# Spatial-gate products over both token chunks, the last expert's last w1 piece in two half loads, its two hidden banks closed one by one, and the final norm's roots behind all sigmoids

## What is computed

```python
# branch A: per head group g (8 of 128 channels) and per chunk of 128 tokens
mixed = jnp.einsum("gts,bnsgc->bntgc", w, v) + b_s.T[:, :, None]
return u * mixed.reshape(bsz, seq, SGU_WIDTH)
...
# 32 experts, top 4 of 32 per token
hid = xb @ w1[e] + b1[e]
glu, lin = jnp.split(hid, 2, axis=-1)
glu = jnp.minimum(glu, SWIGLU_LIMIT)
lin = jnp.clip(lin, -SWIGLU_LIMIT, SWIGLU_LIMIT)
act = glu * jax.nn.sigmoid(SWIGLU_ALPHA * glu) * (lin + 1)
return act @ w2[e] + b2[e]
...
hp = rms_norm(x, ple_norm[i])
x = x + jax.nn.sigmoid(hp @ w_ple_gate[i]) * (p[i] @ w_ple_proj[i])
return rms_norm(x, final_norm)
```

## Time and profile before

| | |
|---|---|
| median of 3 runs | 1232.53 us (1232.52 to 1234.2) |
| the profiled execution's own time | 1233.96 us |
| its span | 1232.2 us |
| TensorE busy | 1201.3 us, 97% of the span |
| VectorE, ScalarE, GpSimd busy | 395.3, 226.7, 45.1 us |
| DMA | 459.51 MB, 90.6% of 16 engines' span |
| chain that ended last | PE 79%, DMA 16%, ACT 2%, DVE 1% |

### The profile page before, as it was taken

The page is one execution under the profiler, slowest core; times in us unless marked ns, Lnnn a source line. Parts: engine busy times, 40 slices in busy tenths (PEclk is TensorE's granted clock), DMA queues, the critical chain, the costliest instruction groups (busy, mean ns, idle before and its releaser), DMA issues.

```text
span 1232.2 us, 15135 instructions
## 1 busy us (share of the span) xinstructions
PE 1201.3 (97%) x6239; PEld 641.4 (52%) x6239; DVE 395.3 (32%) x692; ACT 226.7 (18%) x340; POOL 45.1 (4%) x32
## 2 busy tenths in 40 slices
PE   8999999999999999999999999999999999999987
PEld 7988888875444444444444444444434444444336
DVE  2679954642121111221121111122221111112236
ACT  4766654350000000000000000000000000000018
POOL 6600000010000000000000000000000000000000
PEclk9999999998999999999999999999999999999999
DMA  8655488778999999999999999999999999999990
GB/s 269 203 171 206 137 286 327 275 303 338 425 428 427 430 427 429 429 427 429 429 427 429 429 427 430 428 427 430 428 427 430 426 427 429 427 428 427 428 385 35
DMA packets 62088, 459.51 MB, mean 373 GB/s; under 512 B 7353, under 2 KB 16961, under 8 KB 37218
## 3 DMA queue, kind: packets, MB, share of 16 engines
q1 hardware_dynamic: 62050, 458.95, 90.6%
HBM read 457.87 MB, written 1.06 MB: 372 GB/s over the span
## 4 chain that ended last, share of the span: by engine, by line
PE 79%; DMA 16%; ACT 2%; DVE 1%; issue 1%; SPq 0%; ACTq 0%; DVEq 0%
PE bank L986 28%; PE bank L1035 15%; DMA wring<-in_w_dram 12%; PE bank L948 8%; PE bank L700 5%; PE bank L702 5%; PE bank L701 5%; PE bank L957 4%; DMA vz<-in_w_dram 3%; PE bank L994 1%; DMA blk<-in_w_in_dram 1%; PE bank L756 1%; PE bank L759 1%; PE bank L1016 1%; PE bank L763 1%; PE bank L687 1%
## 5 line engine op out<-in xcount | busy, mean ns | idle before, releaser
L986 PE MATMUL bank<-wring,hT 128*64 128x512 f32 x1376 | 308.2, 597 | 7.0 <-DMA wring<-in_w_dram 6.0
L986 PEld LDWEIGHTS bank<-wring,hT 128*64 128x64 f32 x1376 | 96.3, 137 | 198.6 <-issue 181.6
L1836 DVE TENSOR_SCALAR xbcT<-bank 128x512 f32<-128x512 f32 x32 | 22.1, 692 | 420.5 <-PE bank L994 420.5
L1035 PE MATMUL bank<-wring,xbcT 128*64 128x512 f32 x688 | 154.4, 595 | 1.6 <-DVE hT L1800 1.0
L948 PEld LDWEIGHTS bank<-xbcT,ga 128*128 128x128 f32 x1024 | 122.5, 196 | 3.9 <-DVE xbcT L1795 1.2
L948 PE MATMUL bank<-xbcT,ga 128*128 128x64 f32 x1024 | 121.2, 278 | 0.7 <-DVE xbcT L1795 0.7
L1355 ACT ACTIVATE xbcT<-xbcT 128x512 f32<-128x512 f32 x32 | 20.2, 631 | 504.6 <-DVE xbcT L1836 504.6
L1035 PEld LDWEIGHTS bank<-wring,xbcT 128*64 128x64 f32 x688 | 47.6, 137 | 102.9 <-issue 100.1
L1851 DVE COPY xbcT<-bank 128x256 f32<-128x256 f32 x32 | 13.6, 424 | 272.8 <-PE bank L964 272.8
L1490 DVE TENSOR_TENSOR blk_lo<-blk,blk_hi 128x2048 fp32r<-128x2048 f32 x32 | 73.0, 2288 | 38.7 <-ACT blk_hi L1170 38.6
L1360 ACT ACTIVATE xbcT<-bank 128x512 f32<-128x512 f32 x32 | 19.1, 597 | 346.7 <-PE bank L1035 346.7
(11 more groups left out here) (283 smaller groups left out, 1096.0 us busy)
## 6 DMA issues: line engine op xcount, KB each, us to landing
wring<-in_w_dram SPq DMA_DIRECT2D x129, 2048.0 KB, 33.0
blk<-in_w_dram SPq DMA_DIRECT2D x42, 2048.0 KB, 32.2
vz<-in_w_dram SPq DMA_DIRECT2D x21, 2048.0 KB, 32.9
blk<-in_w_in_dram SPq DMA_DIRECT2D x28, 1024.0 KB, 5.2
blk<-in_w_branch_a_dram SPq DMA_DIRECT2D x4, 1024.0 KB, 5.5
blk<-in_w_branch_b_dram SPq DMA_DIRECT2D x4, 1024.0 KB, 6.6
blk<-in_w_out_dram SPq DMA_DIRECT2D x4, 1024.0 KB, 5.1
x<-in_x_dram SPq DMA_DIRECT2D x4, 512.0 KB, 5.1
```

The costliest lines, as they stand in the source:

```text
L986: last = mm(bank[dh * SLOTS:(dh + 1) * SLOTS, :], xgT[:, k, :], at(c)[:, kk * 2 * F + off + dh * W:kk * 2 * F + off + (dh + 1) * W], start ...
L1035: last = mm(YB[dh * SLOTS:(dh + 1) * SLOTS, :], actT[:, kk * P + c * SLOTS:kk * P + (c + 1) * SLOTS], at(W1C + c)[:, kk * D + dh * W:kk * ...
L1836: ts(g_sb, GLU[:, :], LIMIT, None, ALU.min).then_inc(g_done, 1)
```

## The change

1. **Mixing.** The units become `("mix", q)` for q of 0 to 3. Each holds two head groups over both token chunks: two products with 256 columns instead of four with 128, and VectorE takes each group in one instruction over both chunks.
2. **Last piece of w1.** Piece 3 of the last expert comes in two loads of 1 MB, one per contraction slice, each with a semaphore of its own (`last_half`). TensorE starts on the first slice when the first half is there.
3. **Banks closed one by one.** In every expert, GLU's bias product follows its last contraction slice at once, ahead of LIN's last products, and signals for itself; LIN's follows at the end. VectorE waits for each bank separately.
4. **Tail.** ScalarE does all five sigmoids before the one switch to the square root table; `root(0, 1)` moves behind the last sigmoid. The first 512 columns of both token tiles are now premultiplied on VectorE and scaled on ScalarE, `finish` does columns 512 to 1023 of each tile, and the output goes out in four stores of 256 KB.
5. Semaphores are merged to make room (`eps_set` and `dsel_set` into `small_set`, `pool_step` into `consts`), with the same meaning.

```diff
-    u += [("mix", c, h) for c, h in two]
+    u += [("mix", q) for q in range(SGU_HEADS // 2)]
...
                 sp.wait_ge(chunk_used, g - NSLOT + 1)
-                load_chunk(g)
+                if g == NCH * E - 3:
+
+                    r = (W1C - 1) * RW1 * P
+                    src = w1[0, E - 1, r:r + RW1 * P, :].rearrange("(p k) n -> p k n", k=RW1)
+                    for k in range(RW1):
+                        load(slots[g % NSLOT][:, k * 2 * F:(k + 1) * 2 * F], src[:, k, :], last_half[k])
+                else:
+                    load_chunk(g)
...
             for t in range(TT):
-                sp.wait_ge(out_ready, t + 1)
-                if t:
-                    sp.wait_ge(half_ready, 1)
-                sp.dma_start(out[0, t * P:(t + 1) * P, :], xn[:, t, :]).then_inc(stored, 16)
-            sp.wait_ge(stored, 16 * TT)
+                for part, ready in ((slice(W, D), out_ready), (slice(0, W), half_ready)):
+                    sp.wait_ge(ready, t + 1)
+                    sp.dma_start(out[0, t * P:(t + 1) * P, part], xn[:, t, part]).then_inc(stored, 16)
+            sp.wait_ge(stored, 16 * 2 * TT)
...
+            for q in range(SGU_HEADS // 2):
+                name = ("mix", q)
+                wait_empty(pe, name)
+                for i in range(2):
+                    g = 2 * q + i
+                    last = mm(bank_of(name)[:, i * TOKENS:(i + 1) * TOKENS], sgu_wT[:, g, :], v[:, :, g * P:(g + 1) * P],
+                              start=True, stop=True)
+                last.then_inc(full(name), 1)
...
                 for c in range(W1C):
-                    arrived(c)
+                    if not (last_one and c == W1C - 1):
+                        arrived(c)
                     for kk in range(RW1):
+                        if last_one and c == W1C - 1:
+                            pe.wait_ge(last_half[kk], 16)
+                        hidden(c, kk, GLU, 0)
+                        if c == W1C - 1 and kk == RW1 - 1:
+                            pe.wait_ge(aux_done, j + 1)
+                            if first:
+                                pe.wait_ge(b1_low, 2)
+                            bias(0, GLU).then_inc(hid_filled, 1)
+                        last = hidden(c, kk, LIN, F)
                     last.then_inc(chunk_used, 1)
-                pe.wait_ge(aux_done, j + 1)
-                if first:
-                    pe.wait_ge(b1_low, 2)
-                for g, bank in enumerate((GLU, LIN)):
-                    last = mm(bank[:, :], esel[:, :], b1_pair[:, g * W:(g + 1) * W], start=False, stop=True,
-                              skip_group_check=True)
+                last = bias(1, LIN)
                 last.then_inc(hid_filled, 1)
...
             sigmoid(0, W, W, 3, banks[2])
+            square(0, W, W, 1, 3)
+            sigmoid(1, W, W // 2, 4, banks[3])
+            square(1, W, W // 2, 1, 4)
+            sigmoid(1, W + W // 2, W // 2, 5, banks[4])
             fn(table_out[:, 6:7], ones[:, 0:1], ACT.Sqrt)
-            square(0, W, W, 1, 3)
             root(0, 1)
-            fn(table_out[:, 7:8], ones[:, 0:1], ACT.Sigmoid)
-            sigmoid(1, W, W // 2, 4, banks[3])
-            sigmoid(1, W + W // 2, W // 2, 5, banks[4])
-            fn(table_out[:, 0:1], ones[:, 0:1], ACT.Sqrt)
-            square(1, W, W // 2, 1, 4)
             square(1, W + W // 2, W // 2, 2, 5)
             root(1, 2)
...
-            act.wait_ge(x3_rstd, TT)
-            act.wait_ge(spread_done, 1)
-            fn(xn[:, 1, 0:W], sg[:, 1, 0:W], ACT.Copy, scale=rstd3[:, 1:2]).then_inc(half_ready, 1)
+            for t in range(TT):
+                act.wait_ge(x3_rstd, t + 1)
+                act.wait_ge(spread_done, t + 1)
+                fn(xn[:, t, 0:W], sg[:, t, 0:W], ACT.Copy, scale=rstd3[:, t:t + 1]).then_inc(half_ready, 1)
...
-                dve.wait_ge(hid_filled, j + 1)
+                dve.wait_ge(hid_filled, 2 * j + 1)
                 ts(g_sb, GLU[:, :], LIMIT, None, ALU.min).then_inc(g_done, 1)
+                dve.wait_ge(hid_filled, 2 * j + 2)
                 ts(lin_sb, LIN[:, :], LIMIT, -LIMIT, ALU.min, ALU.max).then_inc(loop_step, 1)
...
             dve.wait_ge(x3_done, 2)
-            tt(sg[:, 1, 0:W], x[:, 1, 0:W], fnorm[:, 0:W], ALU.mult).then_inc(spread_done, 1)
+            for t in range(TT):
+                tt(sg[:, t, 0:W], x[:, t, 0:W], fnorm[:, 0:W], ALU.mult).then_inc(spread_done, 1)
             dve.wait_ge(x3_sq, 2)
             ts(part3[:, 0:1], ssq3[:, 0, 0:1], 1.0 / D, RMS_EPS, ALU.mult, ALU.add).then_inc(x3_part, 1)
             embedded(0, W, W, 3)
-            dve.wait_ge(x3_root, 1)
-            nc.vector.reciprocal(rstd3[:, 0:1], rstd3[:, 0:1]).then_inc(x3_rstd, 1)
-            dve.wait_ge(x3_rstd, 1)
-            dve.wait_ge(x3_done, 3)
-            finish(0, slice(0, D))
             embedded(1, W, W // 2, 4)
-            embedded(1, W + W // 2, W // 2, 5)
             dve.wait_ge(x3_sq, 4)
             link(tt(part3[:, 1:2], ssq3[:, 1, 0:1], ssq3[:, 1, 1:2], ALU.add))
             ts(part3[:, 1:2], part3[:, 1:2], 1.0 / D, RMS_EPS, ALU.mult, ALU.add).then_inc(x3_part, 1)
+            embedded(1, W + W // 2, W // 2, 5)
```

More of the change, by code:

```diff
@@ L332, in build @@
         ssq_done = sem("ssq_done")
-        eps_set = sem("eps_set")
+        small_set = sem("small_set")
         root_done = sem("root_done")
@@ L382, in build @@
         loaded = [sem(f"loaded{i}") for i in range(NSLOT)]
+        last_half = [sem(f"last_half{k}") for k in range(RW1)]
         chunk_used = sem("chunk_used")
@@ L730, in natural @@
                                 between()
[L732 removed]
+            pe.wait_ge(consts, 2)
             pe.wait_ge(mix_loaded, 16)
@@ L979, in expert, with hidden, bias @@
                 pe.wait_ge(xg_done, j + 1)
+                def hidden(c, kk, bank, off):
+                    k = RW1 * c + kk
+                    for dh in range(2):
+                        last = mm(bank[dh * SLOTS:(dh + 1) * SLOTS, :], xgT[:, k, :],
+                                  at(c)[:, kk * 2 * F + off + dh * W:kk * 2 * F + off + (dh + 1) * W],
+                                  start=(k == 0), stop=False, skip_group_check=True)
+                    return last
+                def bias(g, bank):
+                    return mm(bank[:, :], esel[:, :], b1_pair[:, g * W:(g + 1) * W], start=False, stop=True,
+                              skip_group_check=True)
                 for c in range(W1C):
-                    arrived(c)
+                    if not (last_one and c == W1C - 1):
+                        arrived(c)
                     for kk in range(RW1):
[L983 to L988, removed]
-                    last.then_inc(chunk_used, 1)
-                pe.wait_ge(aux_done, j + 1)
-                if first:
-                    pe.wait_ge(b1_low, 2)
-                for g, bank in enumerate((GLU, LIN)):
-                    last = mm(bank[:, :], esel[:, :], b1_pair[:, g * W:(g + 1) * W], start=False, stop=True,
-                              skip_group_check=True)
+                        if last_one and c == W1C - 1:
[7 more added lines that the diff above has]
+                        last = hidden(c, kk, LIN, F)
+                    last.then_inc(chunk_used, 1)
+                last = bias(1, LIN)
                 last.then_inc(hid_filled, 1)
@@ L1629, in _ @@
             wait_taken(dve, *all_of("u"))
[L1630 to L1639, removed]
+            for q in range(SGU_HEADS // 2):
+                name = ("mix", q)
+                wait_filled(dve, name)
+                for i in range(2):
+                    g = 2 * q + i
+                    r = ROWS["sgu_b"] + g
+                    cols = u[:, :, g * P:(g + 1) * P]
+                    mixed = bank_of(name)[:, i * TOKENS:(i + 1) * TOKENS].rearrange("p (c n) -> p c n", c=TT)
+                    last = stt(cols, mixed, paramT[:, r:r + 1], cols, ALU.add, ALU.mult)
+                last.then_inc(empty(name), 1)
             weight_low(19)
@@ L1948, in _ @@
             ts(part3[:, 1:2], part3[:, 1:2], 1.0 / D, RMS_EPS, ALU.mult, ALU.add).then_inc(x3_part, 1)
-            dve.wait_ge(x3_root, 2)
-            nc.vector.reciprocal(rstd3[:, 1:2], rstd3[:, 1:2]).then_inc(x3_rstd, 1)
-            dve.wait_ge(x3_rstd, 2)
-            dve.wait_ge(x3_done, 5)
-            finish(1, slice(W, D))
+            embedded(1, W + W // 2, W // 2, 5)
+            for t in range(TT):
+                dve.wait_ge(x3_root, t + 1)
+                nc.vector.reciprocal(rstd3[:, t:t + 1], rstd3[:, t:t + 1]).then_inc(x3_rstd, 1)
+                dve.wait_ge(x3_rstd, t + 1)
+                dve.wait_ge(x3_done, 5 if t else 3)
+                finish(t, slice(W, D))
 _INS = ["x", "p", "mix_norm", "w_in", "sgu_ln_g", "sgu_ln_b", "sgu_w", "sgu_b", "conv_w", "conv_b", "dt_bias", "a_log",
```

18 lines of the change are left out of this document (8 added, 10 removed).

## The result

The changed kernel takes 1235.97 us (median of 20 executions, 1232.19 to 1238.38). The kernel before took 1233.79 us beside it (20 executions, 1231.64 to 1234.85). The ratio is 1.0016, 95% interval [1.001, 1.0023]: slower by about 2 us, clear of the noise though small, where the forecast had 1232.4 us and no change. The profiled execution took 1236.4 us (span 1234.6, clock 0.992), 2.4 us more than that of before.

The account below looks back on a forecast made before the run. The prediction took the stream of expert weight loads to bound the experts' stage. Mixing -0.1 us and three terms of 0 sum to -0.1 us, from the median 1232.53 to 1232.4 us; range 1230.4 to 1234.2.

Parts of the forecast that it names:

- Mixing, on TensorE: Mixing ahead of the experts: 16 records in 3.46 us replace 32 in 3.57 us, so -0.1 us.
- Piece 5: Last expert's w2 products: start 2.1 us sooner, then wait 2.0 us for this load, landing at 1192.35; 0 us at the end.
- piece 5 is there in time: Rival, last expert: the load doesn't hold TensorE up, the 2.1 and 0.28 us gains go through, 1230.0 us; 8%.
- The term of +0.2 us: Other 31 experts: separate bias products add 0.2 us each, covered by TensorE's 1.6 us lead over the loads; 0 at the end.
- clears it before the last piece 3: Six experts with an extra product fall 3.0 us behind; the next three make up 1.4 us each, so 0 at the end.
- The rival of TensorE as the bound: Rival, experts: at +0.73 us each TensorE falls behind the loads, 6.2 us in six experts, giving 1234.8 us; 4%.
- Tail: After the experts: root sooner by 0.3 us, but later copies and stores cancel it; 0 us, bounds -0.6 and +1.2.
- the drain: Last table load on ScalarE: a rule adds about 1.38 us per switch, giving 1233.8 us; given no chance.
- queue up: Rival, end of the kernel: the four stores do not stream, +1.2 us, 1233.6 us; 9%.
- The clock rival: Rival, last expert: TensorE's clock falls to half speed in the 2.0 us wait, 3.65 us more, 1236.1 us; 8%.
- the steps to LIN's close: Last expert: half-width products and biases from 1180.7 us on close LIN's bank at about 1183.05, against 1184.4 before.

Follow-up runs that it names:

- piece 5 in halves: The changed kernel with the old mixing and the last expert's last w2 piece in two half loads; 1232.94 us, ratio 0.9997, and again 1233.05 us, 0.9995.
- the mixing alone: The kernel before with only the new mixing units added; 1236.45 us, ratio 1.0016.

## Why the prediction was wrong

**The sum lacked a term.** "Mixing, on TensorE: -0.1 us" priced the products that go, and was right as far as it went (3.46 us measured). What it left out is that they are also instructions: 32 fewer of them move the code behind, and with it the fetch for the jump's target. Measured: a gap of 2.73 us in the changed kernel's first profile, 2.0 us of it at the end, and about 2 us on the median. The prediction named no jump, and none of its four rivals had this mechanism. Undoing the mixing, leaving out the jump, and padding by 32 instructions each take the loss away; padding the kernel before by 224 makes it. So the place of the code is shown as the cause; the late fetch behind it is inferred from the times of the transfers.

**The starting point** was low as well. Of the 3.6 us between forecast and measurement 1.3 are not of the change: three executions put the kernel before at 1232.53 us, twenty at 1233.79.

**Piece 5**, the core of the forecast, was right: the w2 products' first half came 1.2 us sooner (2.1 forecast; the clock was back 0.6 us later), then came a wait of 1.54 us (2.0 forecast), and the end of the expert didn't move. The rival "piece 5 is there in time" fell with it.

**The other experts.** The term of +0.2 us was mis-sized: an expert takes 28.16 us instead of 27.81, +0.35. Then six experts fall behind by 6 x 0.70 = 4.2 us, with 1.2 us made up in each of the next three, and the step "clears it before the last piece 3" fails by some 0.6 us. With piece 5 whole nothing shows of it, since that wait absorbs it; with piece 5 in halves it costs 0.4 to 0.7 us by the profiles, 1.0 by the ratios. The rival of TensorE as the bound, to which 4% was given at its upper bound of 0.73 us an expert, began to hold at half that price.

**Tail**: 0 was forecast, -0.2 measured in the span, nothing in the comparison. After the last table load of 1.28 us the next instruction again starts 0.01 us later (1227.43 + 1.28 = 1228.71, 1228.72), so the prediction rightly gave the drain no chance. The stores landed in 2.1 to 2.7 us and did not queue up.

**The clock rival** (8%) had the right mechanism in the wrong gap: not in the wait for piece 5, but in two of the three gaps behind the jump, where it costs twice: in the mixing alone the transposes take 3.67 us instead of 1.97, and the gate's products behind them run slow until 1209.6 us.

**Small slips** that changed nothing: the steps to LIN's close add up to 1183.2 us, not 1183.05, and in the rival of TensorE as the bound 6.2 less three times 0.9 is 3.5 us, not 3.

**The range** ended at 1234.2 us, where the kernel before itself reached 1234.93 in later executions: 3 executions are too few for the spread.

## What to carry to other kernels

Where an engine's program has a taken jump on its critical path, an edit ahead of it that changes the number of that engine's instructions can also be an edit of the jump, as here: look for idle time behind it that the profile puts down to an engine long done or to "issue", and for the instruction queue's transfers in short windows. To tell it from a real cost, pad with waits that are already met: as many instructions as the edit removed. A cost hidden behind loads must be summed over the experts that have no slack, then followed to the next place where the engine should catch up.

## What the runs showed of the hardware

TensorE's instructions arrive in transfers of 16 KB. A shift by -32 instructions and one by +224 put 2.7 to 4.2 us of idle time behind the same jump, which fits a period of 256; it comes in some executions of one and the same program and not in others. A wait met long ago took half an instruction of room, by where the transfer fell. The clock ahead of the experts returns anywhere from 284.56 to 288.02 us, also for one kernel (286.64 and 284.56 for the change); why is open.
